# Two short matmuls of each contraction tile issued one tile later, within a weight chunk, in a two-layer hybrid encoder

## What is computed

```python
hn = rms_norm(x, norm_w)
u = jnp.einsum("bsd,dn->bsn", hn, w_in) + b_in
q, k, v, o, z_a, gates, glu_a, glu_b, z_b, g_a, g_b = jnp.split(u, _OFFSETS, axis=-1)
...
y_a = jnp.einsum("bsw,wd->bsd", ya, w_a)
...
y_b = jnp.einsum("bsw,wd->bsd", c, w_b)
merged = jax.nn.sigmoid(g_a) * y_a + jax.nn.sigmoid(g_b) * y_b
return x + jnp.einsum("bsd,de->bse", merged, w_out)
```

## Time and profile before

| what | value |
|---|---|
| median of three runs | 2449.06 us |
| profiled execution, its own time | 2445.96 us |
| span of that execution, first to last instruction | 2444.2 us |
| granted TensorE clock | 1.00 of full speed |
| TensorE matmuls: busy, share, count | 2426.8 us, 99%, 14020 |
| weight loads: busy | 2129.9 us, 87% |
| DVE busy | 1937.3 us, 79% |
| ACT busy | 1362.2 us, 56% |
| DMA, mean over the span | 182 GB/s |

### The profile page before, as it was taken

How to read it: one execution, slowest core, us unless ns; L and a number is a source line. 1 busy time by engine, 2 the same in 40 slices (tenths; PEclk the granted TensorE clock), 3 DMA queues, 4 the chain that set the end, 5 groups by cost and what they waited for, 6 DMA issues and landing times.

```text
span 2444.2 us, 40523 instructions
## 1 busy us (share of the span) xinstructions
PE 2426.8 (99%) x14020; PEld 2129.9 (87%) x14020; DVE 1937.3 (79%) x2891; ACT 1362.2 (56%) x1631; POOL 39.8 (2%) x39
## 2 busy tenths in 40 slices
PE   8999999999999999999999999999999999999998
PEld 6888888888888888888888888888888888888887
DVE  7798989898987886556678888888898877765565
ACT  6655454545465557555566654545454655665554
POOL 1000000000000000000000000000000000000000
PEclk9999999999999999999999999999999999999999
DMA  7666656565655666665656665555555666666654
GB/s 215 173 193 185 178 167 181 171 178 171 178 179 181 198 184 193 190 189 186 194 156 196 195 180 169 181 168 181 168 180 165 195 189 189 180 198 190 189 189 138
DMA packets 447913, 444.87 MB, mean 182 GB/s; under 512 B 17968, under 2 KB 445760, under 8 KB 447808
## 3 DMA queue, kind: packets, MB, share of 16 engines
q1 hardware_dynamic: 447808, 443.74, 60.8%
HBM read 441.59 MB, written 2.10 MB: 182 GB/s over the span
## 4 chain that ended last, share of the span: by engine, by line
PE 99%; DVE 1%; DMA 0%; ACT 0%; issue 0%; ACTq 0%; SPq 0%
PE ps L1405 57%; PE ps L1408 29%; PE ps L1424 5%; PE ps L1426 2%; PE px L1587 1%; PE px L1566 1%; PE px L1477 0%; PE px L1557 0%; PE ps L1633 0%; PE px L1509 0%; PE px L1574 0%; DMA M<-in_x_dram 0%; PE px L1462 0%; PE ps L1635 0%; PE px L1542 0%; DVE X L799 0%
## 5 line engine op out<-in xcount | busy, mean ns | idle before, releaser
L1405 PE MATMUL ps<-Hs,W 128*128 128x512 f32 x4960 | 1546.0, 393 | 0.0
L761 DVE TENSOR_TENSOR W<-RAW,W 128x1024 fp32r<-128x1024 f32 x832 | 1026.5, 1241 | 399.6 <-ACT W L413 398.1
L413 ACT CAST W<-RAW 128x1024 fp32r<-128x1024 f32 x832 | 863.2, 1048 | 814.6 <-PE ps L1408 694.1
L1408 PEld LDWEIGHTS ps<-Hs,W 128*128 128x128 f32 x4960 | 931.3, 188 | 205.5
L1408 PE MATMUL ps<-Hs,W 128*128 128x256 f32 x4960 | 979.0, 279 | 0.0
L1405 PEld LDWEIGHTS ps<-Hs,W 128*128 128x128 f32 x4960 | 752.2, 188 | 4.1 <-issue 3.1
L900 DVE SCALAR_TENSOR_TENSOR ACC<-CP,CWT,ACC 128x256 f32<-128x256 f32 x928 | 389.3, 478 | 1.1
L1405 PE MATMUL ps<-YC,W 128*128 128x512 f32 x1152 | 358.6, 393 | 2.9 <-DVE W L761 2.9
L1408 PEld LDWEIGHTS ps<-YC,W 128*128 128x128 f32 x1152 | 216.4, 188 | 47.7
L1408 PE MATMUL ps<-YC,W 128*128 128x256 f32 x1152 | 227.4, 279 | 0.0
L1424 PE MATMUL ps<-W,Hs 128*128 128x512 f32 x512 | 182.9, 400 | 0.0
(11 more groups left out here) (207 smaller groups left out, 1007.6 us busy)
## 6 DMA issues: line engine op xcount, KB each, us to landing
RAW<-in_w_in_dram SPq DMA_DIRECT2D x640, 512.0 KB, 3.7
RAW<-in_w_a_dram SPq DMA_DIRECT2D x64, 512.0 KB, 3.4
RAW<-in_w_b_dram SPq DMA_DIRECT2D x64, 512.0 KB, 3.4
RAW<-in_w_out_dram SPq DMA_DIRECT2D x64, 512.0 KB, 4.3
M<-in_x_dram SPq DMA_DIRECT2D x2, 1024.0 KB, 7.6
HEAD<-in_b_in_dram SPq DMA_DIRECT2D x8, 256.0 KB, 4.1
out_dram<-M SPq DMA_DIRECT2D x4, 512.0 KB, 3.8
CP<-in_dw_w_dram SPq DMA_DIRECT2D x3, 128.0 KB, 4.6
```

The costliest lines, as they stand in the source:

```text
L413: nc.scalar.copy(WH[:, c, :, :], RAW[:, c, :, :]).then_inc(hi_made, 1)
L761: v.tensor_tensor(WL[:, c, :, :], RAW[:, c, :, :], WH[:, c, :, :].bitcast(F32), ALU.subtract).then_inc(lo_made, 1)
L1405: mm(ps[:, 2 * q + t, :], WH[:, c, kk, t * P:t * P + P], act_in[:, kt, :], start=(kt == 0), stop=False)
L1408: i = mm(ps[:, 2 * q + t, S:2 * S], WL[:, c, kk, t * P:t * P + P], act_in[:, kt, 0:S], start=False, stop=(kt == KT - 1))
```

## The change

In `multiply`, the two shorts of a contraction tile are issued behind the two longs of the next tile of the same chunk. The chunk's first tile issues its longs alone, and after the last tile's longs come the shorts of the last but one and then those of the last. Which matmuls there are, their operands and the flags `start` and `stop` stay as they were.

```diff
-                    for kk in range(KQ):
-                        kt = c * KQ + kk
-                        if made is not None and kt % size == 0:
-                            pe.wait_ge(made, base + (kt // size + 1))
-                        for t in range(2):
-                            mm(ps[:, 2 * q + t, :], WH[:, c, kk, t * P:t * P + P], act_in[:, kt, :],
-                               start=(kt == 0), stop=False)
-                        for t in range(2):
-                            i = mm(ps[:, 2 * q + t, S:2 * S], WL[:, c, kk, t * P:t * P + P],
-                                   act_in[:, kt, 0:S], start=False, stop=(kt == KT - 1))
+                    for step in range(KQ + 1):
+                        if step < KQ:
+                            kt = c * KQ + step
+                            if made is not None and kt % size == 0:
+                                pe.wait_ge(made, base + (kt // size + 1))
+                            for t in range(2):
+                                mm(ps[:, 2 * q + t, :], WH[:, c, step, t * P:t * P + P], act_in[:, kt, :],
+                                   start=(kt == 0), stop=False)
+                        if step > 0:
+                            kt = c * KQ + step - 1
+                            for t in range(2):
+                                i = mm(ps[:, 2 * q + t, S:2 * S], WL[:, c, step - 1, t * P:t * P + P],
+                                       act_in[:, kt, 0:S], start=False, stop=(kt == KT - 1))
                     i.then_inc(multiplied, 1)
```

## The result

| | before | with the change |
|---|---|---|
| median of 17 runs each | 2448.9 us | 2452.79 us |
| lowest to highest | 2445.9 to 2450.66 | 2451.19 to 2454.15 |
| profiled execution, its own time | 2445.96 us | 2453.86 us |
| profiled execution's span | 2444.2 us | 2452.1 us |

The ratio is 1.0015, with a 95% interval of 1.0009 to 1.0022: 3.9 us slower. Neither profile is of a median execution: the one before is as fast as the fastest of the 17, the one after is among the slower ones, so their spans differ by more than the medians.

The account below looks back on a forecast made before the run. The prediction took TensorE's matmul spacing to bound the kernel. Neighbours, weight loads and waits at 0 us each summed to 0 us on the profiled 2445.96 us; with the runs' median 3.1 us above it, the forecast was 2449.0 us, range 2436 to 2474.

Parts of the forecast that it names:

- What bounds the kernel: Whole kernel: TensorE busy 2426.8 of 2444.2 us, so time is the number of matmuls times their start-to-start spacing.
- How many times the change acts, 764 chunks: In multiply: 6112 longs and as many shorts, 8 of each a chunk; 764 chunks at 2.76 us, 86% of the span.
- Neighbours: Within chunks of multiply: two of eight switches between longs and shorts go; the changed order of neighbours costs 0 us.
- my own sign: In the profile after: wrong if a chunk differs from 2.76 us by over 0.006, or TensorE waits appear inside chunks.
- Weight loads: Four shorts in a row within a chunk: successive loads still hide under shorts of 0.115 us; cost 0 us.
- Waits: In multiply: only the xw_lo wait before tile 2 in each layer's first pair moves; cost 0, at most 0.5 us.
- the moved wait: First pair of each layer: xw_lo wait ahead of tile 1's shorts; if binding, at most 0.5 us, 2449.5 us; chance 0.03.
- fewer switches are faster: Chunks of multiply: two switches fewer at 0.008 us each over 764 chunks, 12.2 us less, 2436.9 us; chance 0.20.
- the rhythm breaks: Four longs at a chunk's head, four shorts at its tail: slower spacing, 24.4 us more, 2473.4 us; chance 0.27.
- Its threshold: Average chunk spacing in multiply: growth by 0.0064 us (4.9 us / 764) makes the slower rhythm decide.
- The formula of the Trainium skill: Chunks of multiply: 109 ns a short, 216 a long, 2.60 us a chunk against the trace's 2.76; not trusted.
- a shift of exactly nothing: Whole kernel: the change has no effect, 0 us, forecast 2449.0 us; chance 0.50.

Follow-up runs that it names:

- e2: Against the kernel before: each chunk issues its eight longs, then its eight shorts; 2447.03 us, ratio 0.9988.
- e4: Against the kernel before: long and short matmuls in turn within a chunk; 2482.93 us, ratio 1.0135.
- e13: Chunks 0 and 2 of each pair six longs, six shorts, two longs, two shorts; chunks 1 and 3 eight longs, eight shorts; against before 2454.63 us, ratio 1.0021.
- e11: Against the kernel before, old order: the two shorts of each chunk's third tile take 248 moving columns in place of 256; 2462.16 us, ratio 1.0053.
- e5: Against the kernel before, old order: weight loads in multiply of 32 columns in place of 128, filling 32 output rows; 2473.26 us, ratio 1.0098.
- e6: The change's order with weight loads of 32 columns in place of 128, filling 32 output rows; against the kernel before 2463.61 us, ratio 1.0059.
- e12: Against the kernel before: each chunk issues six longs, six shorts, two longs, two shorts; 2444.91 us, ratio 0.9983.
- e15: Chunk 0 in the change's order, 1 and 3 six longs, six shorts, two longs, two shorts, chunk 2 eight longs, eight shorts; against before 2443.57 us, ratio 0.9977.
- e14: Chunks 0 and 2 of each pair eight longs, eight shorts; chunks 1 and 3 six longs, six shorts, two longs, two shorts; against before 2447.38 us, ratio 0.9989.

## Why the prediction was wrong

- **What bounds the kernel: right.** TensorE's spacing was all that mattered; waits, ACT, DVE and DMA had no part. Two thousand microseconds of chunks times 0.0025 is what the spacing costs.
- **How many times the change acts, 764 chunks: right.** 764 x 0.007 = 5.3 us is near what the two traces' chunks differ by outside the half-clock stretches, 5.5 us.
- **Neighbours, taken at 0 us: this is the step that failed.** It measured 0.007 us a chunk. By my own sign, a chunk more than 0.006 us away from 2.76, I was wrong. I had said in the text that the rows can't show so small a difference, and had put the middle at 0 because the same kinds of steps occur in both orders. e2, e4, e13 and e11 show why that argument doesn't hold: the spacing of two neighbours is no property of the two. The same eight shorts take 0.90 or 0.94 us, and the same alternating chunk 2.79 or 2.83, depending on what ran before. A sum over neighbours has no right value here.
- **Weight loads at 0: right that four shorts in a row are not held up** (0.45 us, as before). But e5 and e6 show that the width of the weights is not without effect: with 32 columns, and so 32 output rows, both orders are slower.
- **Waits at 0: right in the time, not in the reading.** I had said that the moved wait could cost at most 0.23 us where it bound. It did bind once, for 0.1 us in the first pair, and the wait for the next chunk took that up. The waits on DVE's signal, 3.4 us against 2.9, both stand before a chunk's first long.
- **Rival "fewer switches are faster": wrong.** Its evidence, the last pair's 0.353 us, is real, and e4 reproduces it in 350 of its 764 chunks (2.827 / 8 = 0.353), but a line drawn through 8 and 16 switches doesn't lead on to 6, 4 and 2.
- **Rival "the rhythm breaks": right in kind and sign, wrong in size and place.** I gave it 24.4 us by the rates of other patterns, where the change costs 5.3, and put it in the blocks of four, which are no slower in the change's own profile; its loss is between them. Its threshold, 0.0064 us a chunk, was just passed at 0.007.
- **The formula of the Trainium skill.** The Trainium skill, TensorE: Matmul & The Clock Gate, section Back-to-back issue gap, has N/2.4 + 2.5 ns for the gap of isolated matmuls. Added up over a chunk, as I did, that is an estimate of 2.60 us and has no effect of order. The traces have 2.74 to 2.83 for the same 16 matmuls in this order and others, undisturbed; the measurement decides.
- **That the range held the time says little for the reasoning.** It reaches from 13 us under the forecast to 25 us over it, and the 3.9 us came from a term that I had at nothing. I took half the chance for a shift of exactly nothing. With every other pattern in the trace before slower than the settled one, a small loss was the likelier case. But that too would have been no derivation: e12 and e15 are other orders, and they are faster.

What stays open is the mechanism behind the rhythm. The runs show that it exists, that it is carried from chunk to chunk until an interruption, that it depends on order, on moving columns and on the width of the weights (with that of the output), and that the change's price of 0.007 us is gone with 2-byte operands. Which part of TensorE or its reads makes it was not found.

## What to carry to other kernels

When TensorE runs without a gap, a reordering of its matmuls can still move the time by some tenths of a per cent either way, and a sum over neighbours doesn't tell which. Measure one block's length over many blocks in the trace, start to start; check whether it alternates, and if it does, try other arrangements of the same blocks. The good arrangement is tied to the exact widths and loads: the change that costs 4 to 5 us here gained 10 us in the variant with loads of 32 columns. Where single stretches at half clock come and go, the granted clock of each execution has to be looked at before a difference of some us between two medians is read.

## What the runs showed of the hardware that I had not expected

- fp32r matmuls of 512 and 256 moving columns, each with its own 128x128 load, at a granted clock of 1.00: the next matmul starts 0.225 to 0.237 us after a long and 0.112 to 0.124 us after a short, in repeating patterns that are the same to 1 or 2 ns over hundreds of chunks.
- 16 columns less a chunk made the chunk 0.020 us longer (e11). Weights of 32 columns in place of 128, with 32 output rows in place of 128, made it 0.040 us longer (e5).
- Two steady states of the same instruction sequence, 2.741 and 2.746 or 2.773 and 2.767 us a chunk (e13, e14), 2.791 or 2.827 (e4), each lasting until an interruption.
- The clock fell to half for a few microseconds behind the 8x8 matmuls, and behind the first pair's wait of 2.5 us, in some profiles and not in others, worth 1.6 and 1.2 us in the profile after: the chunk at 208 us takes 4.458 us there, and 2.870 at the same place before.
